# First mixture of experts: experts in pairs in plain fp32 (64 + 32 tokens each, on column tiles of TensorE) in place of one expert at a time in three fp32r products

## The reference, cut to what matters

```python
def moe_swiglu(h, router, w_in, w_out):      # 8 experts, D_FF = 3584, all fp32
    top_logit, top_idx = lax.top_k(hf @ router, 2)
    gates = ... softmax of the two, one-hot ...
    for e in range(8):
        gate, up = jnp.split(hf @ w_in[e], 2, axis=-1)       # w_in[e]: 1024 x 7168
        y = y + gates[:, e:e + 1] * ((jax.nn.silu(gate) * up) @ w_out[e])   # w_out[e]: 3584 x 1024
```

## Time and profile before

| | us |
|---|---|
| median of three runs | 2372.87 |
| the profiled execution's own time | 2372.64 |
| its span | 2370.8 |
| PE busy | 2144.1 (90%) |
| DVE busy | 1467.8 (62%) |
| ACT busy | 1164.1 (49%) |
| POOL busy | 692.7 (29%) |

### The profile page before, as it was taken

One profiled execution on the slowest core, in us unless ns is written; L12 is line 12 of the kernel. 1 busy time (PEld: TensorE's weight loads), 2 busy tenths in 40 slices (PEclk: granted clock), 3 DMA queues, 4 the chain that ended last, 5 costly groups with the idle time before them and its releaser, 6 DMA issues.

```text
span 2370.8 us, 27449 instructions
## 1 busy us (share of the span) xinstructions
PE 2144.1 (90%) x11173; PEld 1664.7 (70%) x11173; DVE 1467.8 (62%) x1549; ACT 1164.1 (49%) x1234; POOL 692.7 (29%) x298
## 2 busy tenths in 40 slices
PE   7898999897898699999999999999999486659997
PEld 6575999563785677878787877888888486544442
DVE  6454555224535489898989899888888565440112
ACT  4752444212422366767777676777776354221110
POOL 2000000000000089999999999500000100000000
PEclk9999999998999599999999999999999696859998
DMA  5463555334525289999999999999998541229995
GB/s 187 137 179 124 170 171 176 113 101 146 164 74 173 97 290 363 325 357 330 351 344 341 354 334 363 328 363 333 369 353 318 150 146 44 106 87 409 418 420 229
DMA packets 266924, 582.96 MB, mean 246 GB/s; under 512 B 11161, under 2 KB 101930, under 8 KB 254496
## 3 DMA queue, kind: packets, MB, share of 16 engines
q1 hardware_dynamic: 264176, 575.09, 68.6%
q0 software_dynamic: 2608, 5.97, 0.9%
HBM read 579.96 MB, written 1.05 MB: 245 GB/s over the span
## 4 chain that ended last, share of the span: by engine, by line
PE 76%; DVE 8%; ACT 8%; issue 4%; DMA 3%; SPq 0%; POOL 0%; DVEq 0%; ACTq 0%; POOLq 0%
PE ps L419 19%; PE ps L420 19%; PE ps L421 19%; PE ps L1967 5%; ACT whi L444 4%; PE ps L561 3%; PE ps L1991 2%; DVE wlo L452 2%; PE ps L1400 1%; PE ps L1419 1%; DMA raw<-in_rg_w_in 1%; DVE sg L1650 1%; PE ps L1952 1%; PE ps L1934 1%; PE ps L1935 1%
## 5 line engine op out<-in xcount | busy, mean ns | idle before, releaser
L452 DVE TENSOR_TENSOR wlo<-raw,whi 128x2048 fp32r<-128x2048 f32 (+3 forms) x433 | 1034.0, 2397 | 466.3 <-ACT whi L444 463.3
L444 ACT ACTIVATE whi<-raw 128x2048 fp32r<-128x2048 f32 (+3 forms) x433 | 822.4, 1902 | 506.7 <-PE ps L421 438.9
L419 PE MATMUL ps<-whi,xh 128*128 128x512 f32 (+3 forms) x1264 | 477.7, 378 | 12.2 <-DVE xl L519 8.4
L420 PE MATMUL ps<-wlo,xh 128*128 128x512 f32 (+3 forms) x1264 | 469.8, 372 | 0.0
L421 PE MATMUL ps<-whi,xl 128*128 128x512 f32 (+3 forms) x1264 | 468.4, 371 | 0.0
L1869 POOL TENSOR_SCALAR y<-y,dl 128x384 f32<-128x384 f32 x120 | 388.1, 3234 | 12.2
L630 POOL DMA_DIRECT2D lnt<-in_ln_gain x4 | 2.2, 550 | 1034.6 <-DVE xl L519 703.3
L419 PEld LDWEIGHTS ps<-whi,xh 128*128 128x128 f32 (+1 forms) x1264 | 240.4, 190 | 56.3 <-DVE xl L519 8.2
L421 PEld LDWEIGHTS ps<-whi,xl 128*128 128x128 f32 (+1 forms) x1264 | 239.7, 190 | 43.5
L420 PEld LDWEIGHTS ps<-wlo,xh 128*128 128x128 f32 (+1 forms) x1264 | 240.6, 190 | 38.8
L1871 POOL TENSOR_TENSOR bias<-bias,y 128x384 f32<-128x384 f32 x120 | 259.4, 2161 | 10.0
(11 more groups left out here) (500 smaller groups left out, 2653.2 us busy)
## 6 DMA issues: line engine op xcount, KB each, us to landing
raw<-in_moe_w_in SPq DMA_DIRECT2D x224, 1024.0 KB, 6.0
raw<-in_moe_w_out SPq DMA_DIRECT2D x112, 1024.0 KB, 5.3
ring<-in_w_gate SPq DMA_DIRECT2D x29, 1024.0 KB, 11.4
raw<-in_ffn_w_in SPq DMA_DIRECT2D x28, 1024.0 KB, 5.2
ring<-in_w_down SPq DMA_DIRECT2D x26, 1024.0 KB, 10.1
raw<-in_w_ada SPq DMA_DIRECT2D x24, 1024.0 KB, 5.2
ring<-in_w_up SPq DMA_DIRECT2D x20, 1024.0 KB, 9.8
raw<-in_ffn_w_out SPq DMA_DIRECT2D x14, 1024.0 KB, 4.9
```

What stands on the lines that cost most here:

```text
L419: e.matmul(o, lh, rh, start=start, stop=False)
L420: e.matmul(o, lh, rl, start=False, stop=False)
L444: e.activation(whi[0:rows, s % NSPL, 0:n], raw[0:rows, i % NRAW, 0:n], ACT.Copy).then_inc(S.hi.s, S.hi.up((s,)))
L452: e.tensor_tensor(wlo[0:rows, s % NSPL, 0:n], raw[0:rows, i % NRAW, 0:n], whi[0:rows, s % NSPL, 0:n].bitcast(F32), ALU.subtract).then_inc( ...
```

## The change

The first mixture takes the form of the second, with room for 96 tokens per expert:

- Experts are taken in four pairs. Tokens 0 to 63 of both experts stand on 64 columns each (the *main* part), tokens 64 to 95 on 32 columns each (the *overflow* part). `CAP1 = 96`; `sel` is 256 columns wide (64 + 64 + 32 + 32, and the last 64 again).
- All products with weights are plain fp32 straight from the landed chunk. For each 128 rows of contraction PE does the main matmuls and then four overflow matmuls of 32 columns, each on its own 32 PSUM partitions of one further bank. There is no hi/lo split of weights (lines 444 and 452 for 336 chunks) and none of the activations.
- The column groups are 1024, 1024, 1024 and 512 wide (`GROUPS`), in chunks of 4 KB pieces (2 KB for the last group); `w_out` comes in pieces of 8 KB.
- Weights come through a ring of 11 slots (`load_ring`, `SLOTS1`); a slot is free when PE has used its chunk.
- `Y` is no longer held in PSUM over the mixture: each pair is scattered into banks taken for it and DVE adds them to h (`gather_out`). The overflow's scatter uses row tiles of 64 rows.
- DVE's `dve_rel` and POOL's `pool_rel` work in `lnt` and `h[:, 2]` in place of `y`, `rb`, `dl`; the middle stage waits for POOL's mark ("bias").

The core of the diff:

```diff
+NRING1, NMORE1, CAP1 = 11, 1, 96
+GROUPS = [(0, 1024), (1024, 1024), (2048, 1024), (3072, 512)]
...
+        def part(x, i):
+            sel = w["sel"][:, x % 2]
+            p = bk.take(e, key, "part", x, i)
+            for k in range(2):
+                for t in range(2):
+                    o, a = p[:, 192 * k:192 * k + 192], 256 * i + 128 * k
+                    e.matmul(o, w["hh"][:, t, a:a + 128], sel[:, t, 0:192], start=t == 0, stop=False)
+                    ins = e.matmul(o, w["hl"][:, t, a:a + 128], sel[:, t, 0:192], start=False, stop=t == 1)
...
+        def scatter(x):
+            e.wait_ge(C.dve.s, C.dve.at(key, "yl", x, 1))
+            e.wait_ge(C.dve.s, C.dve.at(key, "yol", x))
+            for t in range(2):
+                p = [bk.take(e, key, "Y", x, t, q) for q in range(2)]
+                for q in range(2):
+                    for i, n in enumerate(("yh", "yl")):
+                        e.matmul(p[q][:, :], w["selT"][:, x % 2, t, :], w[n][:, 512 * q:512 * q + 512], start=i == 0, stop=False)
+                for i, n in enumerate(("yoh", "yol")):
+                    for q in range(2):
+                        r = slice(64 * q, 64 * q + 64)
+                        ins = e.matmul(p[q][:, :], w["selT"][r, x % 2, 2 + t, :], w[n][r, :], start=False, stop=i == 1)
...
+            for gi, (o, n) in enumerate(GROUPS):
+                for nm in "gu":
+                    ps_ = [bk.take(e, key, nm, x, gi, b) for b in range(n // 512)]
+                    po = bk.take(e, key, nm + "o", x, gi)
+                    for j in range(n // 256):
+                        m = 2048 // n
+                        both = pair_weights(e, C, SLOTS1, (key, x, nm, gi, j), m)
+                        for k in range(m):
+                            kk_ = m * j + k
+                            for b in range(n // 512):
+                                for v in range(2):
+                                    e.matmul(ps_[b][64 * v:64 * v + 64, :], a[:, kk_, 64 * v:64 * v + 64],
+                                             both[v][:, k, 512 * b:512 * b + 512], start=kk_ == 0, stop=kk_ == 7)
+                            for b in range(2):
+                                for v in range(2):
+                                    c = 2 * b + v
+                                    ins = e.matmul(po[32 * c:32 * c + 32, 0:n // 2], a[:, kk_, 128 + 32 * v:160 + 32 * v],
+                                                   both[v][:, k, n // 2 * b:n // 2 * b + n // 2], start=kk_ == 0, stop=kk_ == 7)
...
+                        if step == 2 and before >= 0:
+                            scatter(before)
+                        if x + 1 < NP1 and step == 10:
+                            choose_sel(x + 1)
+                        if x + 1 < NP1 and 11 <= step < 15:
+                            part(x + 1, step - 11)
+                        if gi and nm == "g" and j == 0:
+                            turn(x, gi - 1)
...
+                both = pair_weights(e, C, SLOTS1, (key, x, "d", 0, j), 2)
                 for i in range(2):
                     f = 2 * j + i
                     for q in range(2):
+                        for v in range(2):
+                            e.matmul(D[q][64 * v:64 * v + 64, :], w["ahm"][:, f, 64 * v:64 * v + 64],
+                                     both[v][:, i, 512 * q:512 * q + 512], start=f == 0, stop=f == 27)
                     for q in range(2):
+                        for v in range(2):
+                            c = 2 * q + v
+                            ins = e.matmul(Do[32 * c:32 * c + 32, :], w["aho"][:, f, 32 * v:32 * v + 32],
+                                           both[v][:, i, 512 * q:512 * q + 512], start=f == 0, stop=f == 27)
```

More of the change, by code:

```diff
@@ L156, in build @@
         wlo = right("wlo", [128, NSPL, CW], F32R)
+    with ExitStack() as own:
+        xg1_ = own.enter_context(nc.sbuf_tensor("xg1", [128, 3072], F32, side="right"))
     right = lambda name, shape, dt=F32: ctx.enter_context(nc.sbuf_tensor(name, shape, dt, side="right"))
@@ new lines, in build, with ring_slots @@
+    lo_at = lambda key: ring[:, M.chunks[M.index[key]][4] % NSPL, :]
+    def ring_slots(nm, last, more, end):
+        split = [i for i in range(last - NRAW, last) if M.chunks[i][4] is not None]
+        out = [(ring[:, 2 * NSPL + i % NRAW, :], ((M.lo, M.chunks[i][4]),)) for i in split]
+        out += [(f((nm, i)), ((pe, "used", M.index[nm, i]),)) for i in (1, 2, 3) for f in (hi_at, lo_at)]
+        out += [(ring[:, 2 * NSPL + i % NRAW, :], ((pe, "used", i),)) for i in range(last - NRAW, last) if i not in split]
+        return out + [(a, ((pe, end), (act, end), (dve, end))) for a in more]
@@ new lines, in build, with load_ring @@
+    SLOTS1 = ring_slots("go", first, [more1[:, i, :] for i in range(NMORE1)], "end_gla")
+    def load_ring(e, C, slots, main):
+        for i, (_, _, _, pieces, _, _) in enumerate(C.S.chunks):
+            slot, before = slots[i % len(slots)]
+            if i >= len(slots):
+                e.wait_ge(C.pe.s, C.pe.at("ring", C.S.name, i - len(slots)))
+            elif main:
+                for sig, *mark in before:
+                    e.wait_ge(sig.s, sig.at(*mark))
+            for dst, src in pieces(slot):
+                e.dma_start(dst, src).then_inc(C.S.raw[i % len(slots)].s, C.S.raw[i % len(slots)].up((i,), by=16))
@@ new lines, in pair_weights, with pair_used @@
+    def pair_weights(e, C, slots, key, m):
+        both = []
+        for u in range(2):
+            i = C.S.index[(*key, u)]
+            n = C.S.chunks[i][2]
+            e.wait_ge(C.S.raw[i % len(slots)].s, C.S.raw[i % len(slots)].at(i))
+            both.append(slots[i % len(slots)][0][:, 0:n].rearrange("p (k n) -> p k n", k=m))
+        return both
+    def pair_used(C, key):
+        return [("ring", C.S.name, C.S.index[(*key, u)]) for u in range(2)]
+    NP1 = 4
+    xg1 = xg1_.rearrange("p (b k n) -> p b k n", b=2, k=8)
@@ new lines, in down @@
+        def down(x):
+            turn(x, 3)
+            e.wait_ge(C.pe.s, C.pe.at(key, "D", x))
+            if x:
+                e.wait_ge(C.pe.s, C.pe.at(key, "scat", x - 1))
+            e.wait_ge(C.act.s, C.act.at(key, "gs", x))
+            for q in range(2):
+                e.activation(w["yh"][:, 512 * q:512 * q + 512], bk(key, "D", x, q)[:, :], ACT.Copy,
+                             scale=w["gs"][:, x % 2, 0:1]).then_inc(C.act.s, C.act.up((key, "yh", x, q)))
+            e.activation(w["yoh"][:, :], bk(key, "Do", x)[:, :], ACT.Copy, scale=w["gs"][:, x % 2, 1:2]).then_inc(
+                C.act.s, C.act.up((key, "yoh", x)))
@@ L2871, in build @@
     M.again()
+    R1.again()
     R2.again()
```

613 lines of the change are left out of this document (231 added, 382 removed).

## The result

The changed kernel takes 2378.03 us (median of 20 runs, 2374.21 to 2382.63) against 2373.73 us for the kernel before (20 runs, 2368.50 to 2377.89): a ratio of 1.0021, 95% interval 1.0013 to 1.0028, so 3.1 to 6.6 us slower. Forecast were 16 us. The direction was right and the time lies in the range, but most of the forecast's size is not there. By the prediction's own bands (2366 to 2380 is "same", with a chance of 0.12) 2378 is even no change; it takes 20 runs on each side to tell these 0.2% from nothing.

What follows compares the result with a forecast made beforehand. PE was taken to bound the kernel. 1034.6 + 2.7 - 1024.5 + 2.2 + 1.3 = +16.3 us on 2372.64 gave 2389 us, own range 2360 to 2430; the 8-in-10 range was 2283 to 2465.

Steps and rivals of the forecast that it cites:

- rival 2: Overflow matmuls on PE: four 32-column matmuls run only two at a time, 288 us more, 2677 us; chance 0.16.
- rival 1: Mixture on PE: changing between 64 and 32 columns costs nearly nothing, so 2282 to 2346 us; chance 0.28.
- changes of size: Between 64- and 32-column tiles in 92 blocks per pair: 0.29 us there and back, 26.7 us per pair, 106.9 in all.
- the rule on changing the tiling mode: PE between tile sizes: changing the tiling mode, not just the tile, drains TensorE; 0.10 us applied 184 times per pair.
- DMA: Weight loads in the first mixture: 88.1 MB per pair at 337 GB/s in 261 us, staying hidden.
- bank stalls: At the `u` products, PE waits two or three times per pair for silu to empty a bank: 10.6 us in all.
- the tail: Behind the mixture: copies one after the other and a scatter with two further changes, 8.3 us for 7.0, +1.3.
- further round: Rival: a second round runs because an expert exceeds 96 tokens, over 1000 us more; chance nearly 0.
- Splits gone: worth nothing, PE hid them.: DVE's and ACT's splitting of weights lay beside PE's work, so removing it gains nothing by itself.
- What lies around it, in front: Ahead of the mixture: `choose` has 12 DVE instructions instead of 2 (+1.4), PE 12 more small products (+0.8): +2.2 us.
- the half clock at the start, +2.7 us: First 5 us of the mixture's products run at half clock, where passes cost double: 2.7 us added.
- the mixture's own sum: First product to last in the first mixture: 1034.6 us, with 2.7 added for half clock, against 1024.5 before.

Runs made afterwards that it cites:

- experiment 1: Changed kernel with all main matmuls of a step first, then all its overflow matmuls; 2322.59 us, ratio 0.9783.
- experiment 2: Changed kernel with steps alternating main then overflow, next step overflow then main; 2304.09 us, ratio 0.9695.
- experiment 4: Changed kernel with overflow matmuls on 64 columns instead of 32, in the same places; 2571.07 us, ratio 1.083.
- experiment 3: Changed kernel with both steps' main matmuls, then both overflow parts, alternating in units of two steps; 2288.73 us, ratio 0.9644.
- experiment 6: Kernel before the change, with the first mixture's three leading splits moved out of the stage ahead; 2366.59 us, ratio 0.9968.
- experiment 7: Changed kernel with 669 more VectorE instructions in the first mixture's further rounds, which are jumped over; 2377.61 us, ratio 1.0010.

## Why the prediction was right in direction and too large

**Right, by its steps.** The stage is bound by PE and stays so. Four 32-column matmuls run together (rival 2 is false: 8 passes in 1.06 us). A change of tile size there and back costs 0.29 us (rival 1 is false), and experiments 1, 2 and 4 show that it is the change: without it no gap, with half of it 14.4 us less per pair for 14.5. Counted in the traces, with those to and from 128 columns, a pair has 198, 98, 66 and 40 changes of size in the changed kernel and in experiments 1, 2 and 3, and takes 260.1, 245.8, 241.3 and 237.5 us: 0.14 to 0.15 us for each change throughout. By the rule on changing the tiling mode that the prediction quotes from the Trainium skill, page "TensorEngine Tiling (Array Packing)", each such change drains PE; the trace agrees in so far as each leaves a gap, 0.29 us for two. A pair was forecast at 261 us and took 260.1. DMA was forecast at 337 GB/s and hidden, and did 340. The bank stalls are at the `u` products, but only six in the mixture where two or three per pair were forecast, 6.7 us for 10.6. That the tail is 1.0 us longer for 1.3 is luck: in eight of the nine variants it is 2.4 to 3.7 us longer, as the clock falls ahead of the scatter, which the prediction did not have. No further round ran.

**Wrong: "Splits gone: worth nothing, PE hid them."** This is the step that failed. It was read from a stretch in the middle of the mixture, and holds there. But three splits of the mixture's chunks were issued in the stage ahead, and there ACT and DVE were on the path. Experiment 6 prices them at 6.2 us. For "What lies around it, in front" the prediction has +2.2 us; without the splits it is +2.5, as said, and with them -3.7.

**Wrong: the half clock at the start, +2.7 us.** The first stretches of the changed kernel, in the columns of rows 2:

```profile
800.00:803.00 3.00, 3.00 (x16) 3.00 (x16) 2.83 (x14) 0.67 (x3) 0.00 (x0) 0.50 0.02 5
803.00:806.00 3.00, 3.00 (x17) 2.85 (x16) 2.16 (x30) 0.98 (x2) 0.65 (x1) 0.61 0.01 3
806.00:809.00 3.00, 2.16 (x13) 0.73 (x16) 0.00 (x0) 1.77 (x2) 2.81 (x3) 1.00 0.01 3
```

And of the kernel before, around its first product at 815.12:

```profile
812.00:815.00 3.00, 2.27 (x11) 2.08 (x10) 0.00 (x0) 1.19 (x2) 0.00 (x0) 0.50 0.00 0
815.00:818.00 3.00, 2.88 (x7) 2.36 (x8) 0.00 (x0) 0.00 (x0) 0.00 (x0) 0.50 0.02 5
818.00:821.00 3.00, 3.00 (x9) 2.35 (x8) 0.00 (x0) 0.33 (x1) 0.00 (x0) 0.53 0.00 0
```

In the changed kernel PE was busy without a pause in the gather and the clock rose from 1.2 to 2.4 GHz just ahead of the first product; before it rose only at 820.8 us, and that cost stood only in the time that I compared with. I had taken over the kernel before's half clock without asking where the new sequence would be when it rises. All profiles have it so: in the ten of this form the clock rises 1.1 to 2.8 us ahead of the first product, in the two of the old form (the kernel before and experiment 6) 5.7 and 4.6 us behind it. That the pauses in the old gather are the reason was not tried by itself.

**Slightly too large: the mixture's own sum.** First product to the end of the last is 1031.0 us; forecast 1034.6 and the 2.7. The 3.6 left are 0.9 us per pair; PE's bank stalls (6.7 instead of 10.6) cover them alone.

**Not foreseen: the jump.** 3.1 us in the last stage, in code that the prediction called untouched. The trace of before has the jump with its 1.41 us, but no row of it tells that the same jump can take 3.1 us more.

Put together: 16.3 less 6.2 (splits), plus 0.3 (selection), less 6.3 (clock and sum), less 0.3 (tail), plus 3.1 (jump) is 6.9 us; measured are 3.1 to 6.6. The trace's sum is thus at or above the top of what the runs show, and with the tail as most profiles have it, it would be some 2 us more. What makes up for these 0.3 to 6 us stays open; single profiles, from which the terms are read, differ by up to 7.4 us in stretches of identical code.

**The larger miss is one of use, not of size.** The prediction priced the changes of size at 107 us, more than any other difference in it, and stopped there. An order in which the products of two steps stand together (experiment 3) keeps every product and gives 89 us of it back.

## What to carry to other kernels

Where matmuls of two tile sizes alternate on PE, multiply the number of changes by 0.15 us and put like next to like: here the order alone was worth 89 of 2378 us, and the ring's depth and DMA's rate (412 GB/s, 209 to 215 us per pair) tell how far that goes. "Hidden" is a statement about a stretch: when work goes away, look at every stage in which it was issued, the one ahead of its own above all, and ask there what stood behind it in the engine's order. And when two profiles are set against each other, subtract first what stretches of identical code differ by, here 4.55 us ahead of the stage in question.

## What the runs showed of the hardware that I had not expected

- The jump in the last stage costs VectorE 0.57 us or 3.4 to 4.2 us from the branch to the next instruction, by where it stands in the engine's program: 0.57 in both kernels with the old place and in both that were padded back to it, 3.43 to 4.19 in the eight others. All of them jump over the same rounds. VectorE's jump behind the first mixture takes 3.2 to 3.4 us in all twelve, also over 669 instructions more (3.32 in experiment 7), so a longer jump is not by itself a slower one. The Trainium skill, page "Advanced Engine Details and Errata", section Control Flow Timing, gives a compare-and-branch some 108 ns; the records of the branches themselves are 0.06 to 0.07 us long here, so nearly all of either gap lies behind the branch.
- POOL's operations on 128x384 take 1.57 and 1.00 us when VectorE is idle and took 3.23 and 2.16 us beside its 128x2048 subtractions; 128x272 operations of VectorE left them at 1.62 and 1.02, and took 0.68 us themselves for 0.44 alone.
- Forecast, but in no row of before: four 32-column fp32 matmuls of 512 columns run in one round of 0.86 us, as two of 64 columns do, so tiles of either size fill PE equally; eight passes in 1.06 us. Their first passes start within 0.03 us, and their second ones 0.45 us later, so no tile's second pass holds up another tile's first.
- In a short group of matmuls behind a wait of PE the clock makes the difference: the scatter behind the last pair, after 2.9 to 3.0 us of idle PE, took 3.2 us from its first start to its last in the two profiles where the clock stayed at 1.00 and 4.4 to 5.7 us in the eight where it fell.
